# Order of the first loads in the projection phase of a decoder-layer kernel

## Chip, cores and metric

The kernel runs on one core of a Trainium2 chip. The metric is the device time of one execution in microseconds (us); lower is better. Three runs of the kernel before the change took 1774.41, 1775.65 and 1776.18 us, the median is 1775.65 us.

## What is computed

One inference step of one decoder layer, for a prompt of 256 tokens and for 8 sampled sequences of one token each, 264 tokens in all, model width 2048, everything in fp32:

```python
p = einsum('bld,de->ble', x, w_in)                 # 2048 -> 6680: retention q,k,v,gate; NSA q; six K/V groups; gate logits
ret = silu(rg) * groupnorm(chunk_retention(rope(rq), rope(rk), rv, state))
kc, vc = compress(all cmp_k rows, w_cmp_k), compress(all cmp_v rows, w_cmp_v)   # 64 rows -> 1, each row weighted
o_cmp, imp = attend(q, kc, vc)                     # compressed branch
o_sel = attend(q, the 16 best blocks by imp)       # selected branch
o_win = attend(q, last 512 rows)                   # window branch
feats = [ret | g0*o_cmp + g1*o_sel + g2*o_win]
h = LN1(alpha*x + feats @ w_o)
y = LN2(alpha*h + moe(h))                          # 32 experts in 4 groups, top 2, d_expert 512
```

For the 8 samples `cmp_k` and `cmp_v` lie in pages of 128 rows in a pool of 160 pages; a page table of 8 x 16 numbers says which page is whose. Compressing them means reading every used page, scaling each row and summing 64 rows. The outputs are y for both groups, all new K/V rows, the window buffers and the retention states.

## The kernel before

Three phases follow one another with a barrier between them: `phase_f` (projection of all 264 tokens, the whole attention of the prompt, compression of the samples' pages), `phase_s` (attention of the samples), `phase_m` (output projection, router, experts). The change touches `phase_f` alone.

In `phase_f` every engine has its own written-out program, and semaphores join them. Work is staged by tile `n` of 128 output columns: `N_TILES` is 52, two tiles make a pair of 256 columns, and `GROUP_COLS` gives the order of the 26 pairs (K/V groups first, tiles 0 to 11; NSA queries, tiles 12 to 19; retention from tile 20). x, transposed, lies in SBUF as 16 blocks of the 2048 input rows (`x`, 16 x 264 per partition). A tile is 16 products in fp32, block k of weights times block k of x, into PSUM bank `n % 2`; PE runs blocks 0 to 7 (`half(n, 0)`), then small work that belongs to earlier tiles, then blocks 8 to 15 (`half(n, 1)`).

Weights come in pairs into a ring of three slots, each pair in two DMAs, one per half of the 2048 rows (1 MB, pieces of 1 KB). The sync engine (SP) issues first the two halves of x (1.08 MB each, `loaded[0]`, `loaded[1]`), then the pairs (`w_full[slot][part]`); from the fourth pair on it waits until PE is through with the slot.

ScalarE issues the constants of this phase (`const_p`, 1.59 MB: identity, masks, rope tables), then waits for a memset and issues `w_gl` (gate logit weights, 192 KB in 2048 pieces of 96 bytes), four small loads of `w_cmp_k` and `w_cmp_v`, `gn_g` (1024 pieces of 4 bytes) and four stores of zero rows (128 pieces of 1 KB each). Only then begins its loop over tiles, whose first act is `take_tile(0)`: the copy of tile 0 out of PSUM (L358), which raises `a_free`.

PE, from tile 1 on, puts a rotation (`rotate`, L658) between the two halves of a tile. The first one waits for the constants and for `a_free` at 1:

```python
if not last_tile:
    half(n, 0)
if n == 1:
    pe.wait_ge(S["consts_in"], 16)
if 1 <= n <= 6:
    p, kv = (n - 1) // 2, (n - 1) % 2
    pe.wait_ge(S["a_free"], n)
    rotate(kt[:, p, kv] if p < 2 else ck_t[:, kv], n - 1)
```

Tile 2 needs `a_free` at 1 too, since it writes the bank of tile 0.

GpSimd clears two small tiles, issues twelve small loads around the page table, waits until VectorE has made row numbers of them (`rows_ready`), and then gathers the pages in 32 units: unit u takes eight of the 64 row weights (`wsl`, 128 x 4 KB, for every second unit) and 128 rows of 8 KB by an indirect DMA (`gath`, two buffers). From unit 2 on it waits until VectorE has used the buffer. VectorE pools a unit in `pool_unit` (L563, L565, L566: one multiply over 128x2048, three adds, one more add), one unit at the end of its turn `n`, by the condition `units` (L629). In turns 13 to 20 VectorE also runs the prompt's attention: rope (L473 to L476), `shares`, two copies, then `peaks` (L497 to L506), which waits for PE's scores (L680 to L683).

Of the kernel before, what the change touches and what calls it, by code (L numbers as in the profile page):

```python
# [26 lines left out]
KT = D // P  # L27
# [185 lines left out]
N_TILES = 2 * len(GROUP_COLS)  # L213
Q_TILE, R_TILE = 12, 20
# [8 lines left out]
def phase_f(nc, a, o, m, sem):  # L223


    arena, ps, ft, cst = m.arena, m.ps, m.xt, m.cst
    _, CP = constants()[0]
    c_ = lambda n, r=P: cst[0:r, CP[n][0]:CP[n][0] + CP[n][1]]
    ident = c_("ident")
    take = Taker(arena, 0, KVC)  # L230
    ring = take(FRONT_SLOTS, KT, 2 * DH)
    x = take(KT, T)
# [30 lines left out]
    S = {n: sem(n) for n in names.split()}  # L263
    loaded = [sem("loaded0"), sem("loaded1")]
    w_full = [[sem(f"w_full{j}_{part}") for part in (0, 1)] for j in range(FRONT_SLOTS)]
# [11 lines left out]
    with nc.Block() as block:  # L277
        @block.sync
        def _(sp):
            for part in (0, 1):  # L280
                sp.dma_start(x[:, 8 * part:8 * part + 8, :],
                             a["x_t"].rearrange("p (k t) -> p k t", k=KT)[:, 8 * part:8 * part + 8, :]).then_inc(loaded[part], 16)
            for pair, col in enumerate(GROUP_COLS):
                if pair >= FRONT_SLOTS:
                    sp.wait_ge(S["tile_done"], 2 * (pair - FRONT_SLOTS) + 2)
                for part in (0, 1):
                    k8 = slice(8 * part, 8 * part + 8)
                    sp.dma_start(ring[:, pair % FRONT_SLOTS, k8, :], w_in[:, k8, col:col + 2 * DH]).then_inc(w_full[pair % FRONT_SLOTS][part], 16)
            sp.wait_ge(S["gath_free"], N_UNITS)
            sp.wait_ge(S["wsl_free"], N_UNITS // 2)  # L290
            for b in range(N_WIN):
                window_in(sp, a, m, b)

        @block.gpsimd
        def _(pool):
            pool.memset(zero, 0.0).then_inc(S["zero_ready"], 1)
            pool.memset(w_gl, 0.0).then_inc(S["zero_ready"], 1)
            for g in (0, 1):
                src = a["page_table"][4 * g:4 * g + 4, :].rearrange("s n -> (s n)").unsqueeze(1).unsqueeze(2)
                pool.dma_start(page_of[:, g:g + 1], src.broadcast_to([64, 2, 1])).then_inc(S["rows_in"], 16)  # L300
            pool.dma_start(half_of[:, 0:8], a["half_of"]).then_inc(S["rows_in"], 16)
            for s in range(NS_TOK):
                pool.dma_start(m.seq_row[:, s:s + 1], a["page_table"][s].unsqueeze(1).unsqueeze(2).broadcast_to([NPAGE, 8, 1])
                               ).then_inc(S["rows_in"], 16)
            pool.dma_start(eighth, a["eighth_of"]).then_inc(S["rows_in"], 16)
            pool.wait_ge(S["rows_ready"], 1)
            for u in range(N_UNITS):
                kind, rows8, g = u // 16, u // 2 % 8, u % 2
                if g == 0:
                    if u >= 4:  # L310
                        pool.wait_ge(S["wsl_free"], u // 2 - 1)
                    pool.dma_start(wsl[:, u // 2 % 2], a[("w_cmp_k", "w_cmp_v")[kind]][rows8 * 8:rows8 * 8 + 8, :]
                                   .unsqueeze(0).broadcast_to([P, 8, DH])).then_inc(wsl_in[u // 2 % 2], 16)
                if u >= 2:
                    pool.wait_ge(S["gath_free"], u - 1)
                at = (g * 4 + rows8 // 2) * 2 + rows8 % 2
                pool.indirect_dma_start(
                    out=gath[:, g].rearrange("p a b -> p (a b)"), out_offset=None,
                    in_=a[("cmp_k", "cmp_v")[kind]].rearrange("r (a c) -> (r a) c", a=2),
                    in_offset=bass.IndirectOffsetOnAxis(ap=unit_row[:, at:at + 1], axis=0),  # L320
                ).then_inc(gathered[g], 16)
            pool.wait_ge(S["n_out"], H)
            pool.wait_ge(S["kv_out"], 160)
            pages_in(pool, a, m, 0)
            pages_in(pool, a, m, 1)
            for b in (2, 3):
                pool.wait_ge(S["tile_done"], N_TILES - 8 + 2 * b)
                pages_in(pool, a, m, b)

        @block.scalar  # L330
        def _(act):
            A = nc.scalar
            act.dma_start(cst[:, 0:a["const_p"].shape[1]], a["const_p"]).then_inc(S["consts_in"], 16)
            act.wait_ge(S["zero_ready"], 2)
            act.dma_start(w_gl[:, :, 0:NGL], a["w_gl"].rearrange("p (k n) -> p k n", k=KT)).then_inc(S["gl_in"], 16)
            for t in (0, 1):
                act.dma_start(wrep[t * CB:(t + 1) * CB, 0, :], a["w_cmp_k"]).then_inc(S["wrep_in"], 16)
# [64 lines left out]
            for n in range(N_TILES + 3):  # L402
# [38 lines left out]
                if n >= R_TILE + 6:  # L441
                    r, j = (n - R_TILE) // 8, (n - R_TILE) % 8
# [22 lines left out]
        def _(v):  # L465
# [4 lines left out]
            def rope_low(xt, n, keep):  # L470

                v.wait_ge(S["rotated"], n + 1)
                v.tensor_tensor(n_tmp[0:32], ps[0:32, 6, 0:T], sin_n, ALU.mult)  # L473
                done.link(v.tensor_tensor(xt[0:32], xt[0:32], cos_n, ALU.mult))
                done.link(v.tensor_tensor(xt[0:32], xt[0:32], n_tmp[0:32], ALU.add))
                return v.tensor_copy(keep, xt[:, NP_TOK:T])  # L476
# [108 lines left out]
            for n in range(N_TILES + 3):  # L585

                if 1 <= n <= 6:
                    p, kv = (n - 1) // 2, (n - 1) % 2
                    rope_low((kt[:, p, kv] if p < 2 else ck_t[:, kv]), n - 1, kv_rows[KV_COLS[p]](kv)).then_inc(S["k_roped"], 1)
                if Q_TILE + 1 <= n < R_TILE + 1:  # L590
                    i = n - Q_TILE - 1
                    rope_low(q_t[:, i % 3], 6 + i, by_head(G_Q)[:, i]).then_inc(S["n_roped"], 1)
                if Q_TILE + 2 <= n < R_TILE + 2:
                    shares(n - Q_TILE - 2)
                if Q_TILE + 3 <= n < R_TILE + 3:
                    v.wait_ge(S["n_pt"], n - Q_TILE - 2)
                    v.tensor_copy(prob_t[:, 512:768], ps[:, 5, 0:256])
                    v.tensor_copy(prob_c[0:4, :], ps[0:4, 5, 256:512]).then_inc(S["v_pt"], 1)
                if n == 9:
                    v.wait_ge(S["tok_in"], 4)  # L600
                    for k in (0, 1):
                        last = v.tensor_tensor(
                            cw[:, k].rearrange("p t (k d) -> p (t k) d", d=DH),
                            tok[:, 2 + k].rearrange("p t (k d) -> p (t k) d", d=DH),
                            wrep[:, k].unsqueeze(1).broadcast_to([P, 2 * KV, DH]), ALU.mult)
                    last.then_inc(S["cw_ready"], 1)

                r, j = (n - R_TILE) // 8, (n - R_TILE) % 8
                late = n >= R_TILE + 5
                if late and j == 5:  # L610
                    masked(2 * r)
                if late and j == 6:
                    masked(2 * r + 1)
                if n < N_TILES and v_reads[n]:
                    rope_full(n)
                if late and j == 5:
                    states(2 * r)
                if late and j == 6:
                    normed(2 * r)
                    states(2 * r + 1)  # L620
                if late and j == 7:
                    normed(2 * r + 1)
                    gated(2 * r)
                if late and j == 0:
                    gated(2 * r - 1)

                if Q_TILE + 1 <= n < R_TILE + 1:
                    peaks(n - Q_TILE - 1)
                units = 1 if 2 <= n < 11 or R_TILE < n < N_TILES and j not in (5, 6) else 0  # L629
                for _ in range(units):  # L630
                    pool_unit(pooled)
                    pooled += 1
# [215 lines left out]
def pages_in(pool, a, m, i):  # L848

    name, b = (("sel_k", i) if i < NS_TOK else ("sel_v", i - NS_TOK))  # L850
    pool.indirect_dma_start(out=m.pages[i % 4].rearrange("p a b -> p (a b)"), out_offset=None, in_=a[name],
                            in_offset=bass.IndirectOffsetOnAxis(ap=m.seq_row[:, b:b + 1], axis=0)).then_inc(m.page_full[i % 4], 16)


def window_in(sp, a, m, i):

    name, b = (("win_k", i) if i < NS_TOK else ("win_v", i - NS_TOK))
    sp.dma_start(m.windows[:, i % N_WIN, :], a[name][b].rearrange("(p j) c -> p (j c)", j=4)).then_inc(m.win_full[i % N_WIN], 16)
# [1226 lines left out]
```

## Time and profile before

| | us |
|---|---|
| median of three runs | 1775.65 |
| lowest, highest | 1774.41, 1776.18 |
| span of the profiled execution | 1777.4 |
| PE busy | 1496.4 (84%) |
| VectorE (DVE) busy | 583.0 (33%) |
| ScalarE (ACT) busy | 270.3 (15%) |
| GpSimd (POOL) busy | 68.2 (4%) |
| first matmul | 24.55 |

The span runs from the first to the last instruction of the one execution that was profiled. No time outside the span is given for that execution, so the span stands for its own time; it is 1.75 us above the median of the runs. Busy times don't contain the issuing of DMAs, which the timelines show under ACTq and SPq. The page cuts the span into 40 equal slices of 44.4 us, one digit each; a 9 is nine tenths or more. DMA shares and GB/s are those of the core's 16 DMA engines together. q1 is the queue of SP, q10 that of ScalarE, q0 that of GpSimd; the packets of a queue include the small writes that report a completion.

### The profile page before, as it was taken

To read this page: it belongs to the slowest core of one execution; us is meant where nothing else is said; L and a number is where in the kernel's file an instruction comes from. 1 tells how busy PE (TensorE), PEld (TensorE's weight loads), DVE (VectorE), ACT (ScalarE), POOL (GpSimd) and SP (SyncE) were. 2 spreads that over 40 slices of the span, in tenths; PEclk is the share of its full clock that TensorE was granted. 3 is DMA by queue.
4 is the path that set the end of the run, shared out by engine and by line. 5 is a ranking of instruction groups with operands and counts; after the bars stand their busy time and mean duration, and the time that the engine had idled before them with its cause. 6 is when DMAs were issued, how large, how long until landed. Compare 5 with 4: busy or idle time off the path is not lost.

```text
span 1777.4 us, 25183 instructions
## 1 busy us (share of the span) xinstructions
PE 1496.4 (84%) x10680; PEld 869.9 (49%) x10680; DVE 583.0 (33%) x1240; ACT 270.3 (15%) x618; POOL 68.2 (4%) x88
## 2 busy tenths in 40 slices
PE   4999999999798999958777698967988688787684
PEld 3787788888676577733232233322433223232231
DVE  0744475687554111173321021210212120121026
ACT  0012211201263100021101112111111001101010
POOL 2110000011110000000000000000000000000000
PEclk9999999999898899979898899988999888898895
DMA  8985376786799999329999999999999999999981
GB/s 296 300 299 190 130 260 231 261 299 214 307 366 349 338 284 327 122 79 418 419 420 418 420 419 418 419 419 419 416 419 419 419 420 419 419 419 419 419 368 49
DMA packets 183008, 597.43 MB, mean 336 GB/s; under 512 B 13985, under 2 KB 120033, under 8 KB 126561
## 3 DMA queue, kind: packets, MB, share of 16 engines
q1 hardware_dynamic: 163072, 499.22, 72.4%
q0 software_dynamic: 9792, 75.57, 11.2%
q10 hardware_dynamic: 10024, 20.96, 3.1%
q8 instruction: 87, 1.43, 0.3%
q14 instruction: 33, 0.26, 0.0%
HBM read 586.64 MB, written 17.48 MB: 340 GB/s over the span
## 4 chain that ended last, share of the span: by engine, by line
DMA 36%; PE 22%; DVE 3%; SPq 2%; issue 1%; ACT 0%; ACTq 0%; DVEq 0%
DMA arena<-in_w_up 35%; PE ps L1843 7%; PE ps L1898 5%; PE ps L1928 4%; PE ps L1872 3%; PE ps L1919 2%; SPq L1404 2%; DMA arena<-in_w_down 2%; PE ps L1834 0%; DVE arena L1800 0%; DVE arena L1801 0%; PE ps L1879 0%; SPq L1406 0%; PE ps L1832 0%; ACT arena L1471 0%
## 5 line engine op out<-in xcount | busy, mean ns | idle before, releaser
L1898 PE MATMUL ps<-arena 128*32 128x256 f32 x4352 | 318.1, 439 | 169.4 <-DMA arena<-in_w_up 167.8
L648 PE MATMUL ps<-arena 128*128 128x264 f32 x1664 | 383.0, 388 | 24.6 <-DMA arena<-in_w_in 24.6
L648 PEld LDWEIGHTS ps<-arena 128*128 128x128 f32 x1664 | 313.4, 191 | 78.0 <-issue 26.7
L1898 PEld LDWEIGHTS ps<-arena 128*32 128x32 f32 x4352 | 169.8, 123 | 316.5 <-issue 261.5
L1872 PE MATMUL ps<-arena 128*32 128x512 f32 (+1 forms) x816 | 187.1, 1029 | 4.8 <-DVE arena L1658 4.8
L1706 DVE TENSOR_TENSOR arena<-arena,ps 64x256 f32<-64x256 f32 x34 | 14.4, 425 | 536.3 <-ACT arena L1475 536.3
L1919 PE MATMUL ps<-arena 128*32 128x512 f32 x1088 | 159.5, 690 | 2.9 <-DMA arena<-in_w_down 2.9
L1843 PE MATMUL ps<-arena 128*128 128x264 f32 x512 | 122.2, 397 | 1.4 <-PEq L2036 1.4
L1928 PE MATMUL ps<-arena,keep 128*128 128x512 f32 (+3 forms) x216 | 115.5, 696 | 6.0 <-issue 6.0
L1488 ACT COPY arena<-ps 32x512 f32<-32x512 f32 x136 | 78.3, 576 | 254.2 <-PE ps L1919 253.0
L1843 PEld LDWEIGHTS ps<-arena 128*128 128x128 f32 x512 | 97.7, 194 | 24.2 <-issue 7.8
L1872 PEld LDWEIGHTS ps<-arena 128*32 128x32 f32 (+1 forms) x816 | 30.1, 120 | 114.9 <-issue 106.0
L1919 PEld LDWEIGHTS ps<-arena 128*32 128x32 f32 x1088 | 41.7, 124 | 88.4 <-issue 77.9
L1700 DVE TENSOR_TENSOR arena<-ps,arena 128x512 f32<-128x512 f32 x34 | 23.5, 692 | 186.2 <-PE ps L1879 186.2
L563 DVE TENSOR_TENSOR arena<-arena 128x2048 f32<-128x2048 f32 x32 | 73.3, 2290 | 9.8 <-DMA arena<-in_cmp_k,arena 4.3
L565 DVE TENSOR_TENSOR arena<-arena 128x1024 f32<-128x1024 f32 (+2 forms) x96 | 75.0, 781 | 3.3
L1928 PEld LDWEIGHTS ps<-arena,keep 128*128 128x128 f32 (+3 forms) x216 | 38.4, 185 | 73.8 <-issue 65.5
L1475 ACT ACTIVATE arena<-ps 64x256 f32<-64x256 f32 x34 | 12.8, 375 | 396.1 <-PE ps L1898 396.1
L1713 DVE TENSOR_TENSOR arena<-arena,ps 128x512 f32<-128x512 f32 (+1 forms) x96 | 65.7, 687 | 22.1 <-PE ps L1928 22.1
L1152 PE MATMUL ps<-arena 128*128 128x128 f32 x320 | 47.9, 312 | 2.1 <-ACT arena L988 2.1
L988 ACT COPY arena<-ps 128x512 f32<-128x512 f32 x80 | 41.8, 601 | 31.9 <-PE ps L1152 31.8
L1471 ACT COPY arena<-ps 128x512 f32<-128x512 f32 x34 | 19.9, 585 | 172.4 <-PE ps L1872 172.4
(413 smaller groups left out, 1014.8 us busy)
## 6 DMA issues: line engine op xcount, KB each, us to landing
arena<-in_w_gate SPq DMA_DIRECT2D x128, 1024.0 KB, 26.6
arena<-in_w_up SPq DMA_DIRECT2D x128, 1024.0 KB, 27.0
arena<-in_w_down SPq DMA_DIRECT2D x128, 1024.0 KB, 27.4
arena<-in_w_in SPq DMA_DIRECT2D x52, 1024.0 KB, 6.2
arena<-in_w_o SPq DMA_DIRECT2D x16, 1024.0 KB, 10.9
arena<-in_w_cmp_k POOLq DMA_DIRECT2D x8, 512.0 KB, 8.0
arena<-in_w_cmp_v POOLq DMA_DIRECT2D x8, 512.0 KB, 5.8
arena<-in_win_k SPq DMA_DIRECT2D x8, 512.0 KB, 7.1
```

What stands on the lines that cost most here:

```text
L563: done.link(v.tensor_tensor(x4, x4, wsl[:, u // 2 % 2].unsqueeze(2).broadcast_to([P, 8, KV, DH]), ALU.mult))
L565: done.link(v.tensor_tensor(rows[:, 0:w], rows[:, 0:w], rows[:, w:2 * w], ALU.add))
L648: last = pe.matmul(ps[:, n % 2, 0:T], ring[:, slot, k, cols], x[:, k, :], start=(k == 0), stop=(k == KT - 1))
L988: A.copy(keys_t[:, i % 2, c], ps[:, 5 + n % 3, :]).then_inc(S["s_keys"], 1)
L1152: last = pe.transpose(ps[:, 5 + n % 3, j * P:(j + 1) * P], rows[:, kv * DH:(kv + 1) * DH], ident)
L1488: last = A.copy(ye[first:first + BS, n * CHUNK:(n + 1) * CHUNK], ps[BS * n:BS * n + BS, 4, :])
L1713: v.tensor_tensor(out[:, cols], out[:, cols], ps[R, 5 + u % 3, :], ALU.add).then_inc(S["d_add"], 1)
L1843: last = pe.matmul(ps[:, n % 2, 0:T], ring[:, PLACE[n], k * P:(k + 1) * P], xt[:, k, :], start=(k == 0), stop=(k == KT - 1))
L1872: last = pe.matmul(ps[BS * q:BS * q + BS, 2, :].rearrange("p (a c) -> p a c", a=4), pick[0:n, t, at:at + BS], h_by_k[t][:, 4 * q:4 * q + 4 ...
L1898: last = pe.matmul(ps[BS * q:BS * q + BS, 0, 0:CHUNK // 2], xs[:, kk * 4 + i, :], ring[:, s, at:at + CHUNK // 2], start=(k == 0), stop=(k ...
L1919: last = pe.matmul(ps[BS * n:BS * n + BS, 4, :], hs[:, f % 2, f // 2, :], ring[:, s, n * CHUNK:(n + 1) * CHUNK], start=(f == 0), stop=(f = ...
L1928: return pe.matmul(ps[acc[u // 4][1], bank, :], sel_t[rows, t0:t0 + n], ye[rows, u % 4 * CHUNK:(u % 4 + 1) * CHUNK], start=True, stop=True)
```

## The change

The sync engine now issues half 0 of x, half 0 of pair 0, half 1 of x, half 1 of pair 0, then the constants, then pairs 1, 2 and on. ScalarE issues no constants. Both ScalarE (before `w_gl`) and GpSimd (before the first gather) wait until half 1 of pair 1 has landed. VectorE pools no unit at turns 2 and 3 and one each at turns 14 and 18; the total stays 32.

```diff
--- before.py
+++ after.py
@@ -277,14 +277,15 @@
     with nc.Block() as block:
         @block.sync
         def _(sp):
-            for part in (0, 1):
-                sp.dma_start(x[:, 8 * part:8 * part + 8, :],
-                             a["x_t"].rearrange("p (k t) -> p k t", k=KT)[:, 8 * part:8 * part + 8, :]).then_inc(loaded[part], 16)
             for pair, col in enumerate(GROUP_COLS):
                 if pair >= FRONT_SLOTS:
                     sp.wait_ge(S["tile_done"], 2 * (pair - FRONT_SLOTS) + 2)
+                if pair == 1:
+                    sp.dma_start(cst[:, 0:a["const_p"].shape[1]], a["const_p"]).then_inc(S["consts_in"], 16)
                 for part in (0, 1):
                     k8 = slice(8 * part, 8 * part + 8)
+                    if pair == 0:
+                        sp.dma_start(x[:, k8, :], a["x_t"].rearrange("p (k t) -> p k t", k=KT)[:, k8, :]).then_inc(loaded[part], 16)
                     sp.dma_start(ring[:, pair % FRONT_SLOTS, k8, :], w_in[:, k8, col:col + 2 * DH]).then_inc(w_full[pair % FRONT_SLOTS][part], 16)
             sp.wait_ge(S["gath_free"], N_UNITS)
             sp.wait_ge(S["wsl_free"], N_UNITS // 2)
@@ -304,6 +305,7 @@
                                ).then_inc(S["rows_in"], 16)
             pool.dma_start(eighth, a["eighth_of"]).then_inc(S["rows_in"], 16)
             pool.wait_ge(S["rows_ready"], 1)
+            pool.wait_ge(w_full[1][1], 16)
             for u in range(N_UNITS):
                 kind, rows8, g = u // 16, u // 2 % 8, u % 2
                 if g == 0:
@@ -330,8 +332,8 @@
         @block.scalar
         def _(act):
             A = nc.scalar
-            act.dma_start(cst[:, 0:a["const_p"].shape[1]], a["const_p"]).then_inc(S["consts_in"], 16)
             act.wait_ge(S["zero_ready"], 2)
+            act.wait_ge(w_full[1][1], 16)
             act.dma_start(w_gl[:, :, 0:NGL], a["w_gl"].rearrange("p (k n) -> p k n", k=KT)).then_inc(S["gl_in"], 16)
             for t in (0, 1):
                 act.dma_start(wrep[t * CB:(t + 1) * CB, 0, :], a["w_cmp_k"]).then_inc(S["wrep_in"], 16)
@@ -626,7 +628,7 @@
 
                 if Q_TILE + 1 <= n < R_TILE + 1:
                     peaks(n - Q_TILE - 1)
-                units = 1 if 2 <= n < 11 or R_TILE < n < N_TILES and j not in (5, 6) else 0
+                units = 1 if 4 <= n < 11 or n in (14, 18) or R_TILE < n < N_TILES and j not in (5, 6) else 0
                 for _ in range(units):
                     pool_unit(pooled)
                     pooled += 1
```

## Rows read from the trace of the kernel before

**Rows 1.** The page's 40 slices, busy tenths of PE

```profile
PE   4999999999798999958777698967988688787684
```

**Rows 2.** Waits of PE, 0 to 520 us: total us, times, longest

```profile
PE ps L648 <- DMA arena<-in_w_in: 24.6, 1, 24.6
```

**Rows 3.** The page's chain that ended last, by line, share of the span

```profile
DMA arena<-in_w_up 35%; PE ps L1843 7%; PE ps L1898 5%; PE ps L1928 4%; PE ps L1872 3%; PE ps L1919 2%; SPq L1404 2%; DMA arena<-in_w_down 2%; PE ps L1834 0%; DVE arena L1800 0%; DVE arena L1801 0%; PE ps L1879 0%; SPq L1406 0%; PE ps L1832 0%; ACT arena L1471 0%
```

**Rows 4.** DMA issues near 0.75 and 1.66 us: count, KB each, us to landing

```profile
arena<-in_const_p ACTq DMA_DIRECT2D x1, 1549.5 KB
arena<-in_x_t SPq DMA_DIRECT2D x1, 1056.0 KB, 11.1
...
arena<-in_w_in SPq DMA_DIRECT2D x1, 1024.0 KB, 22.8
```

**Rows 5.** Stretches of the first 30 us; last three columns: granted clock, DMA share, GB/s

```profile
0.00:10.00 10.00, 0.00 (x0) 0.00 (x0) 0.00 (x0) 0.00 (x0) 7.66 (x18) 1.00 0.72 249
10.00:20.00 10.00, 0.00 (x0) 0.00 (x0) 0.00 (x0) 0.00 (x0) 0.00 (x0) 1.00 0.55 192
20.00:30.00 10.00, 5.45 (x14) 4.29 (x15) 1.84 (x7) 0.00 (x0) 3.11 (x4) 1.00 1.10 335
...
4.00:6.00 2.00, 0.00 (x0) 0.00 (x0) 0.00 (x0) 0.00 (x0) 2.00 (x6) 1.00 0.99 410
```

**Rows 6.** Timeline of ScalarE, 0 to 37 us: start, duration, instruction, [idle before]

```profile
1.56 0.66 ACTq L335 DMA_DIRECT2D arena<-in_w_gl  x1
2.25 18.78 ACTq L337 DMA_DIRECT2D arena<-in_w_cmp_k  x1
...
34.77 1.28 ACT L358 ACT_TABLE_LOAD   x1 [34.77 <-issue]
36.06 0.38 ACT L358 COPY arena<-ps 128x264 f32<-128x264 f32 x1
```

**Rows 7.** Timeline of PE, 24 to 46 us

```profile
24.55 13.36 PE L648 MATMUL ps<-arena 128*128 128x264 f32 x48 [24.55 <-DMA arena<-in_w_in]
37.84 0.63 PE L658 MATMUL ps<-arena 32*32 32x264 f32 x2
38.40 7.39 PE L648 MATMUL ps<-arena 128*128 128x264 f32 x32
```

**Rows 8.** Packets by queue: 0 to 21.7; 0 to 34.8; 19 to 28; 28 to 34.8 (two)

```profile
q1 hardware_dynamic: 1336, 3.23, 41.8%
...
q10 hardware_dynamic: 3052, 1.96, 19.3%
...
q10 hardware_dynamic: 2078, 0.26, 19.8%
...
q0 software_dynamic: 347, 2.29, 83.6%
...
q10 hardware_dynamic: 309, 0.07, 4.7%
```

**Rows 9.** Stretch behind the projection (clock 0.50); all matmuls of L648, ns min/median/max

```profile
475.00:480.00 5.00, 0.98 (x5) 0.43 (x3) 4.54 (x6) 0.63 (x2) 0.00 (x0) 0.50 0.18 44
...
L648 PE MATMUL ps<-arena x1664: 386/386/777, 24.6 to 470.5; 128*128 128x264 f32 x185
```

**Rows 10.** Timelines of DVE (one pool unit; tiles 14, 15, 18) and PE (tile 15)

```profile
47.71 2.29 DVE L563 TENSOR_TENSOR arena<-arena 128x2048 f32<-128x2048 f32 x1
...
52.48 0.42 DVE L566 TENSOR_TENSOR arena<-arena 128x256 f32<-128x256 f32 x1
...
152.89 0.17 DVE L506 TENSOR_SCALAR arena<-arena 128x6 f32<-128x6 f32 x1
154.87 0.42 DVE L473 TENSOR_TENSOR arena<-ps,arena 32x264 f32<-32x264 f32 x1 [1.81 <-PE ps L658]
...
192.58 0.42 DVE L473 TENSOR_TENSOR arena<-ps,arena 32x264 f32<-32x264 f32 x1 [3.94 <-PE ps L658]
...
159.25 1.02 PE L680 MATMUL ps<-arena 128*128 128x512 f32 x2
```

## Prediction

> **Bound.** I read the page's slices first: TensorE (PE) is at nine tenths or more from the second slice to the tenth, about 44 to 444 us [rows 1]. The input projection fills that stretch, and it is bound by PE. The waits of PE up to 520 us say the same: in the whole projection one wait for a load is left, 24.6 us before the very first matmul [rows 2]. Later the chain of waits is mostly expert weights arriving, 35% of the span [rows 3]; those stages follow the projection in order, and the edit leaves them alone. So whatever moves the first 60 us moves the end by as much.
>
> What makes the 24.6 us? The first matmul needs half 0 of x and half 0 of weight pair 0. That x half landed 11.1 us after its issue at 0.75, so at 11.9; the weight half 22.8 us after its issue at 1.66, so at 24.5 [rows 4]. The core moved 249 and then 192 GB/s meanwhile, against 410 at its best [rows 5]. The second x half, 1.59 MB of constants (scalar queue [rows 4]) and w_gl, cut into pieces of 96 bytes, stood beside or before the weight.
>
> The other thing to see is ScalarE's queue. It issued w_gl at 1.56, then stood 18.8 us in the issue of a 32 KB load, stood again later, and came only at 34.77 to its first eviction, done at 36.44 [rows 6]. PE was at tile 0 and the first half of tile 1 from 24.55 and reached the first rotation at 37.84 [rows 7]. The rotation reads what that eviction writes. ScalarE beat PE by 1.4 us; that margin is all that hides it.
>
> **The change.** Order on the sync queue: x half, weight half, x half, weight half, constants, then pairs 1 and 2. No bytes are added. PE's start needs 1.08 + 1.05 = 2.13 MB. The run before had moved that many bytes of all kinds at 10 x 2.13/2.49 = 8.6 us [rows 5]. A landing comes 2 to 4 us after the bulk has passed: both x halves and the weight half are 1,280 packets, the sync queue had started 1,336 with its completions at 21.7, and the half landed at 24.5 [rows 4, 8]. So 11 to 16; I take 13, as the twelve small loads of the page table still lie in this stretch. PE would start 11.5 us earlier. Tile 0 and half of tile 1 take 13.3 us [rows 7], so PE is at the rotation at 26.3. The second halves are 2.13 MB more, due about 6 us after the first, when PE's first half is just done: no stall to speak of. The constants are wanted only at the rotation; 5.85 MB had passed at 24.3 by the same sum: little or nothing.
>
> The new wait on ScalarE is for half 1 of pair 1. Up to there the sync queue holds 2.16 (x) + 4.19 (four halves) + 1.59 = 7.94 MB. The run before had moved 2.49 + 1.92 = 4.41 MB at 20 us, and 3.53 MB more at 335 GB/s takes 10.5: 30.5 [rows 5]. Off that goes the w_gl traffic that now comes later, some 1.5; on it the landing, 2 to 4. I take 31. Ends: all of it at 410 GB/s from 2 us on, plus 2, gives 23.5; the sum with the full lag gives 34.
>
> Queued behind this wait on ScalarE are ten DMA issues: one of w_gl, four of the small pooling weights, gn_g, four of zero rows; and behind those the eviction of tile 0. Who waits for that: PE at the first rotation, with it the rest of tile 1, tile 2 and DVE's rope. Were no issue held up, the ten would cost 10 x 0.66 = 6.6 us [rows 6]. They were held up, though: when ScalarE came free its queue had started 3,052 packets, less 128 of constants 2,924. It started them at 2,078/9 = 231 per us beside weights, but at 309/6.8 = 45 per us once the page gathers ran [rows 8]. GpSimd now waits for the same semaphore, so the gathers start with w_gl and not after most of it. GpSimd's first batch is 4 loads x 128 = 512 packets at 347/6.8 = 51 per us, 10 us, in which the scalar queue gets 450. The other 2,470 at 231 per us would be 10.7; with 1.3 for the first packet, 22. Pairs 1 and 2 are through by then and pair 3 waits for PE, so small packets should pass faster than beside weights; no row shows that rate. I take 17, ends 6.6 and 22. ScalarE is free at 31 + 17 = 48. Table load and copy, 1.67 [rows 6], and 0.1: rotation at 49.8 instead of 37.84, +12.0.
>
> PE then has stood from 26.3 to 49.8. What standing costs: behind the idle at the end of the projection the granted clock is 0.50 (1.2 GHz) [rows 9]. At the kernel's start, after 24.55 us of idle, matmuls take up to 777 ns instead of 386, though the clock row reads 1.00 there [rows 5, 9]; 48 took 13.29 us and the next 32 took 7.39, which is 11.1 for 48: 2.2 us lost [rows 7]. That is paid a second time: +2.3, ends 0 (PE doesn't stand) and twice that.
>
> In one place the Trainium skill speaks against this sum: DMA: Bandwidth & Descriptors, section Issuing engines are not separate DMA queues, says that issuing from several engines saves only the sequencer's issue time, usually small beside the DMA itself. By it the ten issues would be the 6.6 us and nothing more. The trace disagrees here: one 32 KB issue held ScalarE for 18.8 us. I make it a rival below.
>
> GpSimd's wait: the first unit was used by DVE at 47.7 [rows 10]. Its gather, issued after 31, lands some ten us later; the first unit is now used at tile 4, 20.5 us after the first rotation, at 70. Hidden by 25 us, by 4 or more if ScalarE isn't late. Nothing else stands behind it on its queue.
>
> Pooling moves from tiles 2 and 3 to 14 and 18, the count before the retention tiles stays 9. Off tiles 2 and 3 nothing is gained: PE didn't wait for DVE there. At tile 14 a unit of 5.2 us follows the peaks, which end at 153.06; the next rope began at 154.87 and would begin at 158.3 [rows 10]. Rope is 1.4, so PE's scores, at 159.25, wait 0.4, and then shares and copies push the values product by 0.8 more. Tile 18 has a pause of 3.94 us ahead of each rope [rows 10]; that takes three quarters of the unit, and its scores come later behind the rope than at tile 15, so it costs nothing. +1.2 in all, ends 0 and 3.
>
> Sum: 12.0 + 2.3 + 1.2 = +15.5. The profiled execution has a span of 1777.4; with it 1792.9. The runs' median is 1775.65, 1.75 below it; the sum is a difference, so the forecast is 1775.65 + 15.5 = 1791 us.
>
> **Rivals.** Issues pass unheld (the skill's rule). ScalarE free at 31 + 6.6 = 37.6, rotation 39.4: +1.6 + 2.3 + 1.2 = +5.1, 1781. For it: the constants are gone from this queue, and w_gl finds it empty. Against it: the loads behind w_gl stood even when the constants had long passed.
>
> The early loads win. The wait for pair 1 ends at 24 to 26 since the stream is undisturbed, the issues take 6.6 to 8, the rotation comes at 32 to 36, and PE stands too short to lose clock: -6 to -2, with the pooling -5 to -1, so 1771 to 1775. It decides where ScalarE comes free before 34. For it: the 410 GB/s of the early stretch. Against it: 249 and 192 were the means, and gathers and w_gl now fall on one spot.
>
> Held longer: the full 22 us and a landing at 34. Rotation at 57.8: +20.0 + 2.3 + 1.2, 1799. That the whole early start passes through (-11.5) is excluded by order: the rotation can't precede the landing of pair 1 and ten issues.
>
> **Numbers.** The forecast with its neighbourhood (1784 to 1796) 0.58; held longer 0.15; unheld issues 0.13, a fifth of it within no change; the early loads win 0.10, half of it a gain that shows; something between, with no change, 0.04. 0.2% (3.6 us) is about what a measurement of this kernel tells from no change. That gives faster 0.06, same 0.10, slower 0.84. Range 1778 to 1800: the ends that the unknown issue time makes, with 1 in 10 below.
>
> **Signs.** PE's first matmul at 11 to 16. ScalarE's first DMA issue at 27 to 34, one of its next issues held for many us, its first copy near 50. PE idle some 20 us ahead of the rotation, then slow matmuls again. PE waits of about 1 us in all for DVE in tile 15. From tile 2 to the end every stage later by the same amount. The forecast is wrong if ScalarE's issues take under 10 us in all, if the gathers no longer slow its queue, or if pair 1 has landed before 26.

## Result and profile after: 0.96% slower, as forecast

The changed kernel takes 1791.78 us (1790.83 to 1792.7, four runs) against 1775.25 of the kernel before measured with it: a ratio of 1.0096, interval [1.0082, 1.011], or +16.5 us. Forecast were 1791 us and +15.5. The times of the experiments were taken on three chips, each beside runs of the kernel before (medians 1776.34 for experiments 1 to 4, 1774.25 for 5 to 7, 1774.58 for 8), so across experiments the ratios are compared and not the times. The page's slices for PE answer to [rows 1]: the projection is as full as before, only it starts and ends later.

```profile
PE   3899999999979799959777789967989677787684
```

PE's waits in the first 520 us of the changed kernel, longest in total first (total us, times, longest of one), answer to [rows 2]. Where one wait for a load stood, there are now two for loads, one for ScalarE of 18.2 us, and two short ones for DVE. The three lines left out stand in both kernels (8.2, 3.5 and 1.5 us here, 8.3, 3.5 and 2.1 before):

```profile
PE ps L660 <- ACT arena L360: 18.2, 1, 18.2
PE ps L650 <- DMA arena<-in_w_in: 17.1, 2, 14.6
...
PE ps L713 <- DVE arena L600: 0.7, 1, 0.7
PE ps L682 <- DVE arena L478: 0.5, 1, 0.5
```

The timeline of ScalarE (start, duration, instruction, idle before) answers to [rows 6]. The first issue comes at 33.17, when pair 1 has landed; the second is held 9.9 us; the eviction of tile 0 begins at 49.96, where it began at 36.06:

```profile
33.17 0.68 ACTq L337 DMA_DIRECT2D arena<-in_w_gl  x1
33.88 9.90 ACTq L339 DMA_DIRECT2D arena<-in_w_cmp_k  x1
...
45.80 0.61 ACTq L341 DMA_DIRECT2D arena<-in_gn_g  x1
46.44 1.19 ACTq L345 DMA_DIRECT2D out_p_wk<-arena  x2
47.66 0.98 ACTq L345 DMA_DIRECT2D out_p_wv<-arena  x2
48.67 1.28 ACT L360 ACT_TABLE_LOAD   x1 [48.67 <-issue]
49.96 0.38 ACT L360 COPY arena<-ps 128x264 f32<-128x264 f32 x1
```

The timeline of PE answers to [rows 7]. It starts ten us earlier, waits 2.47 for the second halves, and then stands from 32.3 to 50.49. The next tile's 32 matmuls take 10.23 us instead of 7.39:

```profile
14.60 6.32 PE L650 MATMUL ps<-arena 128*128 128x264 f32 x16 [14.60 <-DMA arena<-in_w_in]
23.38 8.91 PE L650 MATMUL ps<-arena 128*128 128x264 f32 x32 [2.47 <-DMA arena<-in_w_in]
50.49 1.05 PE L660 MATMUL ps<-arena 32*32 32x264 f32 x2 [18.19 <-ACT arena L360]
51.47 10.23 PE L650 MATMUL ps<-arena 128*128 128x264 f32 x32
61.63 0.63 PE L660 MATMUL ps<-arena 32*32 32x264 f32 x2
```

The granted clock in stretches of the same kernel (PE busy and matmuls, clock, DMA share, GB/s) shows why. This time the record has the lower level itself: 0.50 (1.2 GHz) while PE stands and for its first matmuls after:

```profile
28.00:33.00 5.00, 4.29 (x20) 1.00 1.08 345
33.00:38.00 5.00, 0.00 (x0) 0.88 1.10 322
40.00:50.00 10.00, 0.00 (x0) 0.50 0.79 273
50.00:55.00 5.00, 4.51 (x10) 0.50 0.00 0
55.00:60.00 5.00, 5.00 (x19) 0.78 0.11 27
```

From there the two traces run in parallel. Matmul for matmul the changed kernel is late by 12.65 us at the first rotation, 15.9 at the second, 15.9 through to tile 14, 17.4 after tile 15, and 17.5 at the end of the projection. The spans differ by only 13.4 (1790.8 and 1777.4), four less. From the last matmul of the projection to the first of the output projection the changed kernel's profile is 2.9 us shorter than the one before, and the rest, 1.2, lies behind. No experiment touches that phase either, and in the eight profiles this part was between 1.2 us longer (6) and 5.5 us shorter (7) than in the profile before, with no order by how late PE came to it; I take it for scatter between single executions. In every run with both numbers the time is 1.7 to 1.9 us above the span. By that the execution profiled before stood some 3.9 us above its median (an estimate from 1777.4 + 1.8), and the one after 0.8, which is the three us between 13.4 and 16.5. The medians tell the size.

### The profile page after: what moved, and what is told of

Read it like the earlier page. It is cut to its first block, busy times and chain, and to the rows that moved or that the text cites. A ratio compares the mean times of both kernels' runs of the same rounds, so it can differ in the third digit from the quotient of the medians.

```text
span 1790.8 us, 25185 instructions
## 1 busy us (share of the span) xinstructions
PE 1498.4 (84%) x10680; PEld 868.4 (48%) x10680; DVE 583.1 (33%) x1240; ACT 269.5 (15%) x618; POOL 68.2 (4%) x88
## 4 chain that ended last, share of the span: by engine, by line
DMA 31%; PE 25%; SPq 5%; DVE 2%; issue 1%; ACT 1%; ACTq 0%; DVEq 0%
DMA arena<-in_w_up 29%; PE ps L1900 6%; PE ps L1845 6%; PE ps L1930 5%; PE ps L1874 4%; SPq L1406 4%; PE ps L1921 3%; DMA arena<-in_w_down 2%; SPq L1408 1%; PE ps L1881 1%; PE ps L1836 0%; DMA arena<-in_b_r 0%; ACT arena L1473 0%; DVE arena L1802 0%; DVE arena L1803 0%
## 5 line engine op out<-in xcount | busy, mean ns | idle before, releaser
L1715 DVE TENSOR_TENSOR arena<-arena,ps 128x512 f32<-128x512 f32 (+1 forms) x96 | 65.7, 687 | 20.9 <-PE ps L1930 20.9
L1154 PE MATMUL ps<-arena 128*128 128x128 f32 x320 | 44.2, 294 | 2.5 <-ACT arena L990 2.5
```

The lines of the kernel that those rows point to most:

```text
L1154: last = pe.transpose(ps[:, 5 + n % 3, j * P:(j + 1) * P], rows[:, kv * DH:(kv + 1) * DH], ident)
L1715: v.tensor_tensor(out[:, cols], out[:, cols], ps[R, 5 + u % 3, :], ALU.add).then_inc(S["d_add"], 1)
```

## The experiments

**1. ScalarE's wait taken out.** Everything else as in the changed kernel.

```diff
             act.wait_ge(S["zero_ready"], 2)
-            act.wait_ge(w_full[1][1], 16)
             act.dma_start(w_gl[:, :, 0:NGL], ...)
```

> The changed kernel without ScalarE's wait for pair 1 (GpSimd keeps its wait, order and pooling as changed). Theory: the stall at the first rotation (18.2 us of PE idle in the changed kernel) comes from ScalarE beginning its ten DMA issues at 33.2 instead of 1.6. Then ScalarE is free before PE reaches the rotation at 33 to 36 us, the stall is under 3 us, and the time is 1772 to 1778 us. Rival A: the constants or pair 1 on the sync queue hold PE as well; then PE still stands more than 8 us at the rotation and the time stays above 1783. Rival B: w_gl back in the early stream takes the early start away, first matmul at 20 us or later, time like before the change plus the pooling, 1777.

Measured 1772.62 us, ratio to before 0.998 [0.9964, 0.9996]: so this one wait is worth 21 us by the ratios, and without it the kernel is 0.2% faster than before the change. Its ScalarE and PE:

```profile
2.27 16.24 ACTq L338 DMA_DIRECT2D arena<-in_w_cmp_k  x1
...
28.40 1.28 ACT L359 ACT_TABLE_LOAD   x1 [28.40 <-issue]
```

```profile
18.77 13.73 PE L649 MATMUL ps<-arena 128*128 128x264 f32 x48 [18.77 <-DMA arena<-in_w_in]
32.43 0.63 PE L659 MATMUL ps<-arena 32*32 32x264 f32 x2
```

The held issue is still there, but it lies beside PE's wait for the first load. The rotation comes 5.4 us earlier than before the change (32.43, expected 33 to 36) and PE doesn't stand. Rival A (constants and pair 1 hold PE too) is out. Rival B is right in a part: with ScalarE's ten DMAs back in the early stream the first matmul is at 18.8 and not 14.6, so in this order they cost the start 4 us. How much of that is w_gl's was not taken apart. Of the 5.4 us PE keeps 3.9 behind tile 15; the pooling unit at turn 14 takes 1.5.

**2. Gathers behind the small loads.**

```diff
             pool.wait_ge(S["rows_ready"], 1)
-            pool.wait_ge(w_full[1][1], 16)
+            pool.wait_ge(S["gn_in"], 16)
```

> The changed kernel, but GpSimd waits for gn_g (the last small load of ScalarE) before the gathers instead of for pair 1. Theory: page gathers share the DMA engines with the small pieces and stretch ScalarE's issues, 15.5 us from the first issue to the table load. Without them 7 to 11 us, rotation at 43 to 46 instead of 50.5, time 1785 to 1788. Rival A: the 2048 pieces of w_gl set it alone; then it stays 14 to 16 us and the time at 1791 to 1792. Rival B: gathers start too late and DVE waits at tile 4; then a wait of DVE for a gather shows near tile 4 and the time goes up.

Measured 1787.12 us, ratio 1.0057 [1.0041, 1.0074], 0.4% or 7 us below the changed kernel by the ratios. ScalarE's timeline:

```profile
33.30 0.68 ACTq L337 DMA_DIRECT2D arena<-in_w_gl  x1
34.01 4.24 ACTq L339 DMA_DIRECT2D arena<-in_w_cmp_k  x1
...
42.98 1.28 ACT L360 ACT_TABLE_LOAD   x1 [42.98 <-issue]
```

From first issue to table load 9.7 us instead of 15.5, rotation at 44.8, both as expected. So the gathers make 5.8 us of the 15.5. Of the 9.7 left, 6.6 would be the ten issues unheld; the other 3 us are a hold with no gathers there, beside ScalarE's own pieces and the last weights of pair 2, which weren't taken apart. The packets of the queues in the changed kernel (34 to 38, 38 to 44 twice, 44 to 48.7 us: packets, MB, share) show it directly. While gathers fill the DMA engines (q0 at 95%), ScalarE's queue (q10) starts 74 packets per us; when they have fallen to 20%, 448 per us:

```profile
q10 hardware_dynamic: 1153, 0.11, 23.8%
...
q0 software_dynamic: 365, 2.37, 94.7%
q10 hardware_dynamic: 446, 0.04, 5.6%
...
q10 hardware_dynamic: 2104, 0.44, 45.5%
```

**3. Pooling as before.**

```diff
-                units = 1 if 4 <= n < 11 or n in (14, 18) or R_TILE < n ...
+                units = 1 if 2 <= n < 11 or R_TILE < n ...
```

> The changed kernel with the pooling units at turns 2 to 10 again. Theory: the unit at turn 14 costs PE 1.2 to 1.5 us through DVE (waits of 0.5 and 0.7 us); without it the trace shows no PE wait for DVE before the end of the projection, and the time is 1.2 to 1.6 us lower, 1790.3. Rival: the two waits only take up slack that shows elsewhere, no difference, or the first units come before their gathers have landed and cost more than they save.

Measured 1790.04 us, ratio 1.0069 [1.0043, 1.0094]: 1.7 us below the changed kernel by the medians, 5 by the ratios, and the intervals overlap, so the time alone doesn't decide. The trace does: both waits for DVE are gone, and against the kernel before PE's lateness, matmul by matmul, is 15.65 us at tile 2 and still 15.65 at tile 20, where the changed kernel went from 15.91 to 17.43. DVE and PE of the changed kernel at tile 15 show the wait that is gone (the end of the unit, rope, then PE):

```profile
173.65 0.42 DVE L568 TENSOR_TENSOR arena<-arena 128x256 f32<-128x256 f32 x1
174.32 0.42 DVE L475 TENSOR_TENSOR arena<-ps,arena 32x264 f32<-32x264 f32 x1 [0.25 <-DVE arena L568]
...
175.80 1.12 PE L682 MATMUL ps<-arena 128*128 128x512 f32 x2 [0.47 <-DVE arena L478]
...
178.35 1.10 PE L713 MATMUL ps<-arena 128*128 128x256 f32 x4 [0.65 <-DVE arena L600]
```

The unit at tile 18 cost nothing: in the changed kernel the lateness stays 17.43 from tile 16 to tile 25.

**4. The order alone.** Both waits out, pooling as before.

```diff
-            act.wait_ge(w_full[1][1], 16)
...
-            pool.wait_ge(w_full[1][1], 16)
...
+                units = 1 if 2 <= n < 11 or R_TILE < n ...
```

> The order of the sync queue alone (constants on it), both waits out, pooling as before. Theory: the order is worth what comes through to the rotation: first matmul at 14 to 18, ScalarE free about 30 to 36, rotation 33 to 36 instead of 37.8, time 1770 to 1774. Rival A: w_gl and the gathers from 22 us on hold ScalarE, rotation at 38 or later, no gain or a loss, 1775 to 1780. Rival B: PE waits for half 1 and constants as much as it gained at the start.

Measured 1777.83 us, ratio 1.0005 [0.9994, 1.0017]: no change. I had expected a gain, and each of the four numbers missed (first matmul 19.08, ScalarE free at 36.5, rotation 38.32); rival A holds.

```profile
21.65 12.86 ACTq L343 DMA_DIRECT2D out_p_wk<-arena  x2
34.53 1.93 ACTq L343 DMA_DIRECT2D out_p_wv<-arena  x2
36.50 1.28 ACT L358 ACT_TABLE_LOAD   x1 [36.50 <-issue]
```

```profile
19.08 13.90 PE L648 MATMUL ps<-arena 128*128 128x264 f32 x48 [19.08 <-DMA arena<-in_w_in]
38.32 1.05 PE L658 MATMUL ps<-arena 32*32 32x264 f32 x2 [5.34 <-ACT arena L358]
39.30 10.34 PE L648 MATMUL ps<-arena 128*128 128x264 f32 x32
```

PE starts 5.5 us earlier, but the gathers from 22 us on hold ScalarE's zero stores for 12.9 us, and PE stands 5.3 us for the eviction. The next 32 matmuls then take 10.34 us instead of 7.39; the granted clock is 0.50 from 38 to 45 us (PE busy, clock, DMA share, GB/s):

```profile
40.00:45.00 5.00, 5.00 (x13) 0.50 1.08 367
```

So PE is 3.9 us late from tile 2 on, of which the time shows at most 3.0 (the upper end of its interval). Beside experiment 1 this shows that, of the two waits, GpSimd's is the useful one in this order: with it ScalarE is free at 28.4, without it at 36.5.

**5. ScalarE's loads spread, old order.** The kernel before, with the nine later issues moved into the loop over tiles.

```diff
             act.wait_ge(S["zero_ready"], 2)
-            act.dma_start(w_gl[:, :, 0:NGL], ...
...
+            def small_in(n):
+                if n == 1:
+                    act.dma_start(w_gl[:, :, 0:NGL], ...
...
+                if n in (3, 4):
...
+                if n == 5:
...
+                if n in (7, 8):
...
                     take_tile(n)
+                small_in(n)
...
-            v.wait_ge(S["wrep_in"], 64)
-            v.wait_ge(S["gn_in"], 16)
...
+                if h == 0:
+                    v.wait_ge(S["gn_in"], 16)
...
                     v.wait_ge(S["tok_in"], 4)
+                    v.wait_ge(S["wrep_in"], 64)
```

> The kernel before with one thing changed: ScalarE issues only the constants ahead of tile 0; w_gl goes out behind the eviction of tile 1, the pooling weights behind 3 and 4, gn_g behind 5, the zero rows behind 7 and 8 (DVE waits for each where it first reads it). Theory: w_gl stood beside the first weight half, but the first x halves and the constants still do; first matmul at 20 to 23 instead of 24.5, no stall at the rotation, 1772 to 1775. Rival: the start depends on the order alone, no change, or the late small loads hold ScalarE between evictions and PE waits.

Measured 1776.13 us, ratio 1.001 [0.9998, 1.0021]: no change, the theory missed. The first matmul comes at 24.42, without ScalarE's small loads as with them:

```profile
24.42 13.32 PE L655 MATMUL ps<-arena 128*128 128x264 f32 x48 [24.42 <-DMA arena<-in_w_in]
37.67 0.63 PE L665 MATMUL ps<-arena 32*32 32x264 f32 x2
```

So in the old order neither w_gl, with its 2048 pieces of 96 bytes, nor the other small loads of ScalarE held the first weights. And ScalarE having nothing ahead of its first eviction is worth nothing where PE is later.

**6. The same spread, new order.** `small_in` and DVE's waits as in 5, GpSimd's wait and the new order as in the changed kernel, units at 4 to 12.

```diff
-            act.wait_ge(w_full[1][1], 16)
-            act.dma_start(w_gl[:, :, 0:NGL], ...
...
+            def small_in(n):
...
-                units = 1 if 4 <= n < 11 or n in (14, 18) or R_TILE < n ...
+                units = 1 if 4 <= n < 13 or R_TILE < n ...
```

> The changed kernel with ScalarE's ten issues spread over tiles 1 to 8 instead of waiting for pair 1 and standing before tile 0, pooling units at turns 4 to 12. Theory: nothing stands between PE and the rotation but its own work: first matmul at 14.6, a wait of 2 to 4 for half 1, rotation at 32 to 33 (5.4 earlier than before the change), no wait for DVE at tile 15 since turns 11 and 12 take the two units; 1769 to 1771. Rival: w_gl issued behind tile 1 collides with the gathers and holds ScalarE in a later issue, PE waits for an eviction, gain under 3 us.

Measured 1769.87 us, ratio 0.9966 [0.9951, 0.998]: 0.34% faster than before the change, and 23 us below the changed kernel by the ratios. First matmul 14.91, a wait of 2.70 for half 1, rotation at 30.91 without a stall (a little before the 32 to 33 expected), no wait for DVE at tile 15. PE is 6.9 us early from there to the end of the projection.

**7. Page table loads late.** As 6; only pair 0 goes ahead of GpSimd's twelve small loads.

```diff
+            pool.wait_ge(w_full[0][1], 16)
             for g in (0, 1):
                 src = a["page_table"]...
...
+            def row_numbers():
+                v.wait_ge(S["rows_in"], 16 * (4 + NS_TOK))
...
+                if n == 1:
+                    row_numbers()
-                units = 1 if 4 <= n < 13 or R_TILE < n ...
+                units = 1 if 5 <= n < 13 or n == 18 or R_TILE < n ...
```

> As e6, but GpSimd issues its twelve small page table loads only once pair 0 has landed; DVE makes the row numbers at the end of turn 1, units at turns 5 to 12 and 18. Theory: the twelve loads, in pieces of 4 bytes, take engine time from the first loads (the core moved 80 to 240 GB/s from 6 to 13 us in the changed kernel, with the sync queue full); without them x half 0 and weight half 0 land at 9 to 11, half 1 at 15 to 17, rotation at 23 to 27, time 1762 to 1766. Rival A: the dip is the sync queue's own, the first matmul stays at 14 or later and the time at 1769 to 1771. Rival B: gathers come too late, DVE waits at tile 5, gain under 4 us more than e6.

Measured 1761.08 us, ratio 0.9916 [0.9895, 0.9937], the fastest of all and below the 1762 to 1766 expected. First matmul at 9.04, at the early edge of what was expected, rotation at 21.92, earlier than expected.

```profile
9.04 12.95 PE L661 MATMUL ps<-arena 128*128 128x264 f32 x48 [9.04 <-DMA arena<-in_w_in]
```

The stretches of experiment 6, then of 7 (all engines' busy times, clock, DMA share, GB/s) show where it comes from:

```profile
5.00:10.00 5.00, 0.00 (x0) 0.00 (x0) 0.00 (x0) 0.00 (x0) 3.23 (x7) 1.00 0.57 192
10.00:15.00 5.00, 0.09 (x1) 0.12 (x1) 0.00 (x0) 0.00 (x0) 0.00 (x0) 1.00 0.53 193
15.00:20.00 5.00, 5.00 (x13) 3.93 (x14) 0.00 (x0) 0.00 (x0) 0.00 (x0) 1.00 0.72 260
```

```profile
5.00:10.00 5.00, 0.96 (x2) 0.83 (x3) 0.00 (x0) 0.00 (x0) 0.00 (x0) 1.00 1.05 389
10.00:15.00 5.00, 5.00 (x17) 3.87 (x16) 0.00 (x0) 0.00 (x0) 0.20 (x1) 1.00 1.08 384
...
20.00:25.00 5.00, 5.00 (x22) 3.67 (x22) 1.36 (x4) 0.19 (x1) 1.56 (x3) 1.00 0.63 175
```

The dip moves with the twelve loads. In 6 GpSimd issues them from 1.48 us on and the last has landed by 20.9; the dip lies between 5 and 20 us. In 7 it issues them from 14.80 on and the last has landed by 32.3; the dip lies at 20 us and later. There it costs one PE wait of 0.7 us for a load. What it is about these loads was not taken apart: their small pieces, their number, or that GpSimd's queue carries them.

**8. Page table loads late, old order.** The kernel before, its order and ScalarE's block untouched, with the edit of 7.

```diff
+            pool.wait_ge(w_full[0][1], 16)
             for g in (0, 1):
                 src = a["page_table"]...
...
-                units = 1 if 2 <= n < 11 or R_TILE < n ...
+                if n == 1:
+                    row_numbers()
+                units = 1 if 4 <= n < 13 or R_TILE < n ...
```

> The kernel before with its old order and ScalarE's ten issues where they were; only GpSimd's twelve page table loads wait for pair 0, DVE makes the row numbers at the end of turn 1, units at turns 4 to 12. Theory: the page table loads alone held the first loads, whatever the order. Both x halves, constants and w_gl still stand before or beside the weight half: 1,280 packets and the constants at full rate, first matmul at 15 to 17 instead of 24.5; w_gl then passes early, ScalarE is free before 26, rotation at 28 to 31, time 1765 to 1769. Rival A: w_gl beside the weight half takes what is gained, first matmul at 20 or later, time above 1770. Rival B: gathers late, DVE waits at tile 4 and PE with it.

Measured 1764.92 us, ratio 0.9944 [0.9927, 0.996]. First matmul at 16.13 and rotation at 28.54, as expected, the time just below the 1765 to 1769 expected. Rival A, that w_gl beside the weights takes the gain, is out. ScalarE's held issue is down from 18.8 to 10.0 us and is over before PE needs it:

```profile
1.56 0.66 ACTq L336 DMA_DIRECT2D arena<-in_w_gl  x1
2.25 10.00 ACTq L338 DMA_DIRECT2D arena<-in_w_cmp_k  x1
...
18.36 1.28 ACT L359 ACT_TABLE_LOAD   x1 [18.36 <-issue]
25.08 0.38 ACT L359 COPY arena<-ps 128x264 f32<-128x264 f32 x1 [5.44 <-PE ps L653]
```

```profile
16.13 12.48 PE L653 MATMUL ps<-arena 128*128 128x264 f32 x48 [16.13 <-DMA arena<-in_w_in]
```

The eight and the two kernels side by side (us from the profiles, times as medians; each ratio to the kernel before as run beside it). In 5, 6 and 7 none of ScalarE's small DMAs stands ahead of its table load, and it waits there for PE; in the other rows the table load comes when its issues are through:

| kernel | first matmul | ScalarE at its table load | first rotation | time | ratio |
|---|---|---|---|---|---|
| before | 24.55 | 34.77 | 37.84 | 1775.25 | 1 |
| changed | 14.60 | 48.67 | 50.49 | 1791.78 | 1.0096 |
| 1 no wait on ScalarE | 18.77 | 28.40 | 32.43 | 1772.62 | 0.998 |
| 2 gathers later | 16.25 | 42.98 | 44.80 | 1787.12 | 1.0057 |
| 3 old pooling | 14.43 | 49.49 | 51.31 | 1790.04 | 1.0069 |
| 4 order alone | 19.08 | 36.50 | 38.32 | 1777.83 | 1.0005 |
| 5 spread, old order | 24.42 | 34.26 | 37.67 | 1776.13 | 1.001 |
| 6 spread, new order | 14.91 | 27.50 | 30.91 | 1769.87 | 0.9966 |
| 7 and page table late | 9.04 | 18.52 | 21.92 | 1761.08 | 0.9916 |
| 8 page table late alone | 16.13 | 18.36 | 28.54 | 1764.92 | 0.9944 |

The time follows the first rotation, not the first matmul: 4 starts 5.5 us earlier than before and gains nothing. Behind a stall the slower matmuls come on top.

## Why the prediction was right, step by step

- Start of PE: 13 taken, 14.60 measured. In the sum it didn't matter, as said: it is covered by the stall.
- "No stall to speak of" for the second halves was wrong: PE waited 2.47 us, and was at the rotation at 32.3, not 26.3. This too is covered, but in a kernel without the ScalarE stall (6) it counts in full, 2.7 us.
- Landing of pair 1: 31 taken, 33.2 measured.
- Issue time of ScalarE's ten: 17 taken between ends of 6.6 and 22, 15.5 measured. The errors of these two terms, 2.2 us too early and 1.5 too long, nearly cancel, which is luck: ScalarE free at 48 taken, 48.67 measured; rotation 49.8 and 50.49. The value in the middle rested on a guess that small packets pass faster without weights beside them; once the gathers had thinned out they did, 448 per us against 231 [rows 8]. Experiment 2 shows the part of the gathers.
- The Trainium skill's rule (DMA: Bandwidth & Descriptors, Issuing engines are not separate DMA queues), that issue time is usually small, doesn't hold here: 10 issues took 15.5 us, and 9.7 without gathers, against 6.6 unheld. In every run in which w_gl stood straight ahead of the next issue, that issue was held, 4.2 to 18.8 us; where the issues were spread over the tiles (5 to 7), each took 0.3 to 0.8 us, as the rule has it.
- Clock: 2.3 taken, 3.3 measured (rotation to rotation 11.14 us instead of 7.88). Mechanism right, size short by a third. The loss isn't a constant, so one row couldn't size it: behind the stalls of experiments 2 to 4 (13.9, 17.9 and 5.3 us) the same 32 matmuls took 8.87, 9.14 and 10.34 us, against 7.39. The stall of 5.3 us also answers a rival, which had PE stand "too short to lose clock".
- Pooling at tile 14: 1.2 taken, 1.5 measured; tile 18 at nothing, as said. The first unit was used at 79.7 and not at 70: from the first rotation to turn 4 it is some 26 us at full clock, not 20.5. That only adds slack.
- The sum +15.5, the medians +16.5. PE's lateness at the end of the projection is 17.5; what is between lies in phases whose length varies. The three terms measured (12.65, 3.3 and 1.5) all came out above what was taken.
- What the prediction had as the cause of the 24.6 us start was half wrong. It named the x half, the constants and w_gl in front of the weights; experiment 5 takes w_gl away and nothing moves, experiment 8 takes the twelve page table loads away and 8.4 us go. Those twelve the prediction named only as a reason to take 13 and not less.
- The rival "issues pass unheld" failed on size, "the early loads win" on the landing of pair 1. The chances of the parts add up to 0.05 faster, 0.12 same and 0.83 slower, not quite the 0.06, 0.10 and 0.84 given.

Left open: why a ScalarE issue is held, that is, what it waits for in the queue; and why ScalarE's early DMAs cost the first matmul 4 us in the new order (1) and nothing in the old (5). The runs show what stretches it (pieces of its own queue, gathers, page table loads) and not the rule by which it is let go.

## What to carry to other kernels

Before adding a wait to an engine that issues DMAs, list what else stands in that engine's program behind it: here an eviction that PE needed, some 20 us from one line meant for DMA order (1). Judge early loads by the first point where all engines meet, not by the first matmul. And look in the first stretch at every load, not only at those with the most bytes: taking GpSimd's 12 loads with 13 KB in all out of it brought the first rotation forward by 9.3 us (8), the new order of x, weights and constants, with GpSimd's wait and ScalarE's issues spread, by 6.9 (6). Small pieces alone don't tell which load it is: w_gl's 2048 pieces of 96 bytes cost the old order nothing (5).

## What the hardware showed that I had not expected

- Twelve loads with pieces of 4 to 32 bytes, 13 KB in all, kept the core at 192 to 193 GB/s for 10 us in experiment 6, where 7 moved 389 and 384. The DMA share fell with it (0.57 and 0.53 against 1.05 and 1.08), so the engines' recorded packets don't contain the time: it shows as idle.
- One issue of a 32 KB load held its engine 18.8, 16.2, 10.0, 9.9 or 4.2 us, depending on what the DMA engines did meanwhile (before, 1, 8, changed, 2).
- The clock row read 1.00 at the kernel's start while matmuls took up to 777 ns, but 0.50 behind the stall in the middle, where they took up to 809 ns.
